# Earlier transposes of the normed block, and a one-slice cross sublayer in a new order

## The chip, the cores and the metric

One Trainium2 chip, one of its cores. The metric is the device time of the whole program in microseconds (us); lower is better. The core's engines run side by side and synchronise by semaphores: TensorE (PE; its weight loads are listed as PEld), VectorE (DVE), ScalarE (ACT), GpSimd (POOL), and SyncE (SP), which issues the loads of the weights.

## What is computed

Fourteen sublayers over 256 tokens of width 1024, in float32. Each ends with a residual and a layer norm over the whole row:

```
for layer in 0, 1:                      # first block, sublayers 0 to 5
    x = LN(a*x + mixer(x))              # "even" (mLSTM and a neighbourhood attention), then "odd" (differential)
    x = LN(a*x + cross(x, mem))         # 4 heads of 256: softmax(q k^T / 16) v, then @ wo  (1024 x 1024)
    x = LN(a*x + (silu(x@wg) * (x@wu)) @ wd)       # hidden width 2816
for layer in 0, 1:                      # second block, sublayers 6 to 13
    x = LN(a*x + 0.5 * swiglu(x))
    x = LN(a*x + merge(x))              # three gated branches
    x = LN(a*x + cross(x, mem_2))       # 4 heads of 128: wq 1024 x 512, wkv 1024 x 1024, wo 512 x 1024
    x = LN(a*x + 0.5 * swiglu(x))
```

The order is even, cross, ffn, odd, cross, ffn | ffn, merge, cross, ffn, ffn, merge, cross, ffn. All projections keep float32 accuracy: each operand is split into a high part (fp32r) and a low remainder, and a product is three matmuls (high x low, low x high, high x high).

## The kernel before

**Tiles of weights.** A weight tile is 128 x 2048 elements (1 MB; a few are smaller). SyncE loads it to one of three raw buffers, in one fixed order, and waits with a load until the tile three places before it is split. ScalarE makes the high part (wh, L1069) and VectorE the low part (wl, L1510) of each, in the same order. Most tiles go through a ring of three places (wh, wl); a place is rewritten once the tile three before in the ring is used. Beside the ring there are slots in memory that is otherwise free at a time: front, side (in oh, ol), back (in hh, hl), mem and note (em and en). They hold the opening tiles of the next sublayer. ScalarE and VectorE split ahead of need: `get(name)` on either splits every tile up to the one two ring places (`look=PARTS - 1`) behind the newest that was in the ring, or in use, when TensorE's program wrote the result `name`, and then waits for the result. Slot tiles between them in the order are split on the way.

**The end of a sublayer** (`out_proj`). The output is y = (activations) @ W, in two halves of 512 columns, and k runs over 128 rows of W; a step is a tile of four k. The last three steps (in the one-slice cross two steps, which are all) are held: the products of the first block of 128 tokens for all held tiles come first, then those of the second block. So the first block's residual and norm, on VectorE, run beside the second block's products. Then the normed block is transposed on TensorE (`x_to_T`, eight transposes of 128 x 128 for a block, in two halves of four) and split to xh (ScalarE, L1099) and xl (VectorE, L1543).

**The opening of a sublayer** (`enter`), where it isn't a cross sublayer: products of the first block with two or three opening tiles, then of the second block. Nine openings: after the two cross sublayers of the first block (two slices of wo, c = 2), after the two of the second block (one slice, c = 1) and after five ffn. Ffn and merge have three opening tiles, odd has two. Since every opening tile is taken with the first block's parts first, `await_parts` stands ahead of both blocks.

**Cross sublayers.** The memory is transposed and its keys and values are projected at the end of the sublayer before (`cross_kv`). In the one-slice form (sublayers 8 and 12) there are one tile of each half of the queries, two of the keys, two of the values (k 0 to 3 and 4 to 7), two of wo. `cross` then projects the first queries, computes scores of unit 0, projects the second queries, and runs four units (heads) through a pipeline: scores, negated maximum on VectorE (L1651), exponentials on ScalarE (L1144), division on VectorE (L1661), transposes of the probabilities, values, parts oh and ol.

VectorE's residual of the first block begins with `o = get(name, ...)` with a look of two ring tiles, and its second half with a split of all opening tiles:

```
if half and j + 1 in entry_last:
    split_to(entry_last[j + 1])
o = get(name, 0 if t and (half or by_block) and not cross_after(j) else PARTS - 1)
```

Of the kernel before, what the change touches and what calls it, by code (L numbers as in the profile page):

```python
# [9 lines left out]
ALU = mybir.AluOpType  # L10
# [3 lines left out]
P = 128  # L14
D = 1024
KC = D // P
# [4 lines left out]
FFN = 2816  # L21
HC = FFN // P
PAIRS = (HC - 4) // 2
ALPHA = 4.0 ** 0.25
EPS = 1e-5
NEG = -1e30
# [57 lines left out]
def program(nc, ctx, A, out, LAST=14):  # L84
# [160 lines left out]
    weight_tiles = []  # L245
    ring = []
    free_after = {}
    entry_last = {}
    where = {}
    uses = [0] * 8  # L250
    given = [0] * 8
# [85 lines left out]
    def _(pe):  # L337
# [134 lines left out]
        def y_products(j, t, half, k0, kc, sh, sl, tile, ks=None):  # L472
            h, l = tile
            name = ("y", j, t, half)
            o = ps[where[name][0]]
            for k in ks or range(k0, min(k0 + 4, kc)):
                tok = slice(t * P, t * P + P)
                three(o[:, :], sh[:, k, tok], sl[:, k, tok], h[:, k - k0, :], l[:, k - k0, :], k == 0, k == kc - 1,
                      name if k == kc - 1 else None)
# [7 lines left out]
        def out_proj(j, W, kc, sh, sl, need=None, steps=None):  # L487


            if steps is None:  # L490
                steps = [(half, k0) for half in range(2) for k0 in range(0, kc, 4)]
            held = 0 if cross_after(j) else min(PARTS, len(steps))
            enters = j + 1 < LAST and not cross_after(j)
            early, late = entry_slots(j) if enters else ([], [])
            tiles = []
            for half, k0 in steps[:len(steps) - held]:
                if need:
                    need(min(k0 + 4, kc))
                y_step(j, W, half, k0, kc, sh, sl)
                if (half, k0) in ((0, 4), (0, 12)) and enters:  # L500
                    tiles.append(order_entry(j + 1, len(tiles), early.pop(0)))
                if half == 0 and k0 + 4 >= kc and cross_after(j):
                    mem_start[j + 1] = len(halves)
                    mem_to_T(j + 1)
            if enters and kc == HC:
                free_after["back"] = len(ring) - 1
                if early:
                    tiles.append(order_entry(j + 1, len(tiles), early.pop(0)))
            held_tiles = []
            for half, k0 in steps[len(steps) - held:]:  # L510
                if need:
                    need(min(k0 + 4, kc))
                held_tiles.append(y_tile(j, W, half, k0, kc))
                while early or late and (half, k0) == steps[-1]:
                    tiles.append(order_entry(j + 1, len(tiles), (early or late).pop(0)))
                if (half, k0) == steps[-1]:
                    if enters:
                        entry_last[j + 1] = tiles[-1]
                y_products(j, 0, half, k0, kc, sh, sl, held_tiles[-1])
            for i, (half, k0) in enumerate(steps[len(steps) - held:]):  # L520
                ks = list(range(k0, min(k0 + 4, kc)))
                if i == held - 1 and enters:
                    y_products(j, 1, half, k0, kc, sh, sl, held_tiles[i], ks[:-1])
                    x_to_T(j + 1, [0])
                    ks = ks[-1:]
                y_products(j, 1, half, k0, kc, sh, sl, held_tiles[i], ks)
                owed[0] += 1
            if cross_after(j):
                cross_kv(j + 1)
            elif enters:  # L530
                enter(j + 1, tiles)
# [74 lines left out]
        def cross_kv(j):  # L606
# [2 lines left out]
            await_parts()  # L609
            for n in range(2 * c):  # L610
                proj_T(("xk", j, n), [wkv[:, n * S:n * S + S]], KC, mh, ml)
            for half in range(c):
                for k0 in (0, 4):
                    if k0 and half == c - 1:
# [2 lines left out]
                           "acc" if half == c - 1 else "work")  # L617
            for slot in ("mem", "note"):
                free_after[slot] = len(ring)

        def transposed_probs(u, src):
            pe.wait_ge(sig("prob_ready"), unit[0] + u + 1)
# [7 lines left out]
        def cross(j):  # L630
            _, blk, layer, _ = SUB[j]
            _, wq, _, wo, c = cross_of(blk, layer)
            await_parts()
            for n in range(c):
                proj_T(("xq", j, n), [wq[:, n * S:n * S + S]], KC, xh, xl)
# [419 lines left out]
    def _(act):  # L1055
# [60 lines left out]
        def norm(j):  # L1116
            for t in range(TB):
                ahead(("y", j, 1 if cross_after(j) else t, 1), PARTS - 1 if t == 0 or cross_after(j) else 0)
                if j + 1 in entry_last:
# [34 lines left out]
        def softmax(n_units, biased, after, beside=None):  # L1154
# [21 lines left out]
                    after(t - 3)  # L1176
            unit[0] += n_units

        def cross(j):
            c = cross_of(SUB[j][1], 0)[4]  # L1180
            base = unit[0]

            def query(n):
                name = ("xq", j, n)
# [309 lines left out]
    def _(dve):  # L1494
# [76 lines left out]
        def out_proj(j):  # L1571

            _, _, c = norm_of(j)

            def residual(t, half):
                f = slice(half * 512, half * 512 + 512)
                name = ("y", j, t, half)
                if half and j + 1 in entry_last:
                    split_to(entry_last[j + 1])
# [38 lines left out]
            if cross_after(j):  # L1618
                c = cross_of(SUB[j + 1][1], 0)[4]
                for half in range(c):  # L1620
                    if half == c - 1:
                        x_to_T(j + 1)
                    for t in range(TB):
                        name = ("xv", j + 1, t, half)
                        o = get(name)
# [28 lines left out]
        def normalise(g, biased):  # L1654
# [3 lines left out]
            else:  # L1658
# [2 lines left out]
            dve.tensor_tensor(two(prob[:, g % 2, :]), two(prob[:, g % 2, :]), along(rden[:, g % 2, 0:2], S),  # L1661
                              ALU.mult).then_inc(sig("prob_ready"), 1)

        def cross(j):
            c = cross_of(SUB[j][1], 0)[4]
            base = unit[0]

            def after(u):
                name = ("O", base + u)
# [674 lines left out]
```

## Time and profile before

| | |
|---|---|
| three runs | 2366.25, 2378.0, 2381.45 us |
| median | 2378.0 us |
| profiled execution: its time | 2377.74 us |
| profiled execution: span of its instructions | 2375.9 us |
| mean granted clock of TensorE | 0.987 |
| TensorE busy | 2267.1 us (95%) |
| VectorE busy | 1457.9 us (61%) |
| ScalarE busy | 1053.9 us (44%) |
| DMA | 411.68 MB, mean 173 GB/s |

The span is from the first to the last instruction. TensorE's busy time overlaps in itself: a matmul is listed from its start to its modelled end, while the next starts before that. A granted clock of 1.00 is 2.4 GHz, 0.50 is 1.2 GHz.

### The profile page before, as it was taken

Reading aid. Unit: us, or ns where it says so; the run is one execution under the profiler, and the core shown is the slowest. Engines: PE = TensorE matmul, PEld = TensorE weight load, DVE = VectorE, ACT = ScalarE, POOL = GpSimd, SP = SyncE. Lnnn points to the kernel's source line nnn. Section 1 sums busy time; section 2 is a strip of 40 time slices with the busy share of each in tenths; the row PEclk is TensorE's granted clock in tenths of the full one; section 3 lists DMA queues with packets and bytes.
Section 4 is the critical chain, followed back from the end, with each engine's and each line's share of the span. In section 5 each row is a group of like instructions: output and inputs, shape, how many; then the busy total and the mean of one; then the engine's idle time right before and its main releaser. Section 6 shows DMA issues by size and latency. Waiting matters only on the chain. (4 is left out here: it accounts for less than half of the span.)

```text
span 2375.9 us, 38020 instructions
## 1 busy us (share of the span) xinstructions
PE 2267.1 (95%) x15963; PEld 2079.4 (88%) x15963; DVE 1457.9 (61%) x1708; ACT 1053.9 (44%) x1237; POOL 113.1 (5%) x179
## 2 busy tenths in 40 slices
PE   8979999998999999999999998999999999998998
PEld 8858899877888998997998987997997898986996
DVE  6676555568756555555764676555555765676454
ACT  4534444445453443443455444443443455444442
POOL 2130000000000000000011000000000002000000
PEclk9999999999999999999999999999999999999999
DMA  8545556643445665555642663565566553564553
GB/s 251 167 119 197 172 160 196 225 138 107 173 147 178 195 222 161 185 200 168 199 145 83 206 213 125 178 203 187 178 195 209 169 161 100 171 233 137 178 187 115
DMA packets 337753, 411.68 MB, mean 173 GB/s; under 512 B 11244, under 2 KB 269480, under 8 KB 337456
## 3 DMA queue, kind: packets, MB, share of 16 engines
q1 hardware_dynamic: 328480, 377.18, 49.1%
q0 software_dynamic: 9104, 32.06, 4.4%
q8 instruction: 128, 2.10, 0.4%
q14 instruction: 41, 0.34, 0.0%
HBM read 406.31 MB, written 5.00 MB: 173 GB/s over the span
## 5 line engine op out<-in xcount | busy, mean ns | idle before, releaser
L1510 DVE TENSOR_TENSOR wl<-raw,wh 128x2048 fp32r<-128x2048 f32 (+2 forms) x351 | 764.7, 2184 | 521.6 <-ACT wh L1069 423.2
L342 PE MATMUL bank<-xl,wh 128*128 128x256 f32 x3136 | 878.8, 280 | 4.8 <-issue 3.5
L342 PE MATMUL bank<-xh,wl 128*128 128x256 f32 x3136 | 872.6, 278 | 0.0
L342 PE MATMUL bank<-xh,wh 128*128 128x256 f32 x3136 | 872.5, 278 | 0.0
L1069 ACT ACTIVATE wh<-raw 128x2048 fp32r<-128x2048 f32 (+2 forms) x351 | 637.3, 1821 | 332.3 <-PE bank L342 295.8
L342 PEld LDWEIGHTS bank<-xl,wh 128*128 128x128 f32 x3136 | 592.1, 189 | 13.6 <-issue 12.5
L342 PEld LDWEIGHTS bank<-xh,wl 128*128 128x128 f32 x3136 | 593.6, 189 | 0.6 <-issue 0.2
L342 PEld LDWEIGHTS bank<-xh,wh 128*128 128x128 f32 x3136 | 590.8, 188 | 0.0
L342 PE MATMUL bank<-wl,hh 128*128 128x512 f32 x528 | 206.2, 390 | 4.6 <-DVE wl L1510 4.6
L342 PE MATMUL bank<-wh,hh 128*128 128x512 f32 x528 | 205.5, 389 | 0.0
L342 PE MATMUL bank<-wh,hl 128*128 128x512 f32 x528 | 205.5, 389 | 0.0
L342 PEld LDWEIGHTS bank<-wl,hh 128*128 128x128 f32 x528 | 99.1, 188 | 26.4 <-issue 6.2
L342 PEld LDWEIGHTS bank<-wh,hh 128*128 128x128 f32 x528 | 99.1, 188 | 20.5
L342 PEld LDWEIGHTS bank<-wh,hl 128*128 128x128 f32 x528 | 99.1, 188 | 20.0
L1215 ACT ACTIVATE gate_s<-bank 128x512 f32<-128x512 f32 x54 | 32.3, 598 | 184.4 <-PE bank L342 184.4
L342 PE MATMUL bank<-wl,oh 128*128 128x512 f32 x224 | 91.3, 407 | 11.1 <-ACT oh L1099 10.2
L342 PE MATMUL bank<-wh,oh 128*128 128x512 f32 x224 | 89.3, 399 | 0.0
L342 PE MATMUL bank<-wh,ol 128*128 128x512 f32 x224 | 89.1, 398 | 0.0
L1099 ACT ACTIVATE xh<-bank 128x512 fp32r<-128x512 f32 x56 | 30.4, 598 | 112.6 <-PE bank L342 112.6
L1543 DVE TENSOR_TENSOR xl<-bank,xh 128x512 fp32r<-128x512 f32 x56 | 36.1, 686 | 66.9 <-ACT xh L1099 66.9
L2166 POOL DMA_DIRECT2D gb<-in_ln_g x14 | 7.6, 539 | 1376.0 <-DVE x L1614 1376.0
L342 PEld LDWEIGHTS bank<-wl,oh 128*128 128x128 f32 x224 | 43.4, 194 | 22.1 <-ACT oh L1099 11.9
(362 smaller groups left out, 3149.3 us busy)
## 6 DMA issues: line engine op xcount, KB each, us to landing
raw<-in_ffn_w_in SPq DMA_DIRECT2D x80, 1024.0 KB, 5.2
raw<-in_w_mix_in SPq DMA_DIRECT2D x56, 1024.0 KB, 5.4
raw<-in_ffn_w_gu SPq DMA_DIRECT2D x40, 1024.0 KB, 5.2
raw<-in_ffn_w_out SPq DMA_DIRECT2D x40, 1024.0 KB, 5.0
raw<-in_ffn_w_down SPq DMA_DIRECT2D x20, 1024.0 KB, 5.0
raw<-in_mem_wkv SPq DMA_DIRECT2D x16, 1024.0 KB, 6.3
raw<-in_even_w_in SPq DMA_DIRECT2D x14, 1024.0 KB, 7.2
raw<-in_odd_w_in SPq DMA_DIRECT2D x12, 1024.0 KB, 5.3
```

The costliest lines, as they stand in the source:

```text
L342: ins = pe.transpose(o, a, b) if transpose else pe.matmul(o, a, b, start=start, stop=stop)
L1069: act.activation(part_of(t, 0), raw_tile(t), ACT.Copy).then_inc(sig("w_high"), 1)
L1099: act.activation(dst, src, ACT.Copy).then_inc(sig("part_high"), 1)
L1215: free(("gate", j, q), act.activation(gate_s[:, q % 2, :], o[:, :], ACT.Silu))
L1510: dve.tensor_tensor(part_of(t, 1), raw_tile(t), part_of(t, 0).bitcast(F32), ALU.subtract)\
L1543: ins = dve.tensor_tensor(dst, src, hi.bitcast(F32), ALU.subtract)
L2166: pool.dma_start(gb[:, i, :], v.partition_broadcast(P)).then_inc(sig("gains_loaded"), 16)
```

## The change

`out_proj` on TensorE's side: the opening tiles are ordered elsewhere. After an ffn the back tile comes behind the second held tile (before: ahead of all held tiles). In a two-slice cross mem comes behind the first held tile and note behind the second (before: both behind the first). In a one-slice cross mem, note and front all come behind the second, last output tile (before: mem and note between the two). There the first held tile's products wait for their output parts k by k. The transposes of the first normed block come when three k of the second block's products are left (`BESIDE = 3`; before: one k).

`enter`: the transposes of the second block come ahead of the third opening tile of the first block (before: behind it). With two opening tiles nothing changes.

`cross_kv`, one slice: the transposes of x come behind both key tiles and ahead of the first value tile; the second value tile moves to the cross sublayer. `single_cross`: both query tiles, four scores one after the other, the second value tile, transposes of all four units, then all four outputs. Probabilities use prob and logit, transposed ones probT and bm, so that each unit has a buffer. ScalarE begins with a small exponential. ScalarE splits the mem tile between the transposed probabilities and the outputs; VectorE splits mem and note behind the outputs.

```
@@ out_proj on TensorE
             if enters and kc == HC:
                 free_after["back"] = len(ring) - 1
-                if early:
-                    tiles.append(order_entry(j + 1, len(tiles), early.pop(0)))
             held_tiles = []
-            for half, k0 in steps[len(steps) - held:]:
-                if need:
+            for i, (half, k0) in enumerate(steps[len(steps) - held:]):
+                gradual = need and kc == 4 and len(held_tiles) == 0
+                if need and not gradual:
                     need(min(k0 + 4, kc))
                 held_tiles.append(y_tile(j, W, half, k0, kc))
-                while early or late and (half, k0) == steps[-1]:
-                    tiles.append(order_entry(j + 1, len(tiles), (early or late).pop(0)))
-                if (half, k0) == steps[-1]:
+                if i + 1 == held:
+                    for slot in early + late:
+                        tiles.append(order_entry(j + 1, len(tiles), slot))
                     if enters:
-                        entry_last[j + 1] = tiles[-1]
-                y_products(j, 0, half, k0, kc, sh, sl, held_tiles[-1])
+                        entry_tiles[j + 1] = tiles
+                elif early and (i or kc != HC) and kc != 4:
+                    tiles.append(order_entry(j + 1, len(tiles), early.pop(0)))
+                y_products(j, 0, half, k0, kc, sh, sl, held_tiles[-1], need=need if gradual else None)
+            todo = sum(min(k0 + 4, kc) - k0 for _, k0 in steps[len(steps) - held:])
             for i, (half, k0) in enumerate(steps[len(steps) - held:]):
-                ks = list(range(k0, min(k0 + 4, kc)))
-                if i == held - 1 and enters:
-                    y_products(j, 1, half, k0, kc, sh, sl, held_tiles[i], ks[:-1])
-                    x_to_T(j + 1, [0])
-                    ks = ks[-1:]
-                y_products(j, 1, half, k0, kc, sh, sl, held_tiles[i], ks)
+                for k in range(k0, min(k0 + 4, kc)):
+                    if todo == BESIDE and enters:
+                        x_to_T(j + 1, [0])
+                    y_products(j, 1, half, k0, kc, sh, sl, held_tiles[i], [k])
+                    todo -= 1
                 owed[0] += 1
@@ enter
-                if t == 1:
-                    x_to_T(i, [1])
                 await_parts()
                 for m, n in enumerate(tiles):
...
+                    if t == 0 and m == 2:
+                        x_to_T(i, [1])
...
+                if t == 0 and len(tiles) == 2:
+                    x_to_T(i, [1])
@@ cross_kv
+            if c == 1:
+                x_to_T(j)
+                proj_N([("xv", j, t, 0) for t in range(TB)], wkv, 512, 512, KC, mh, ml, [0], "acc")
+                return
@@ TensorE
+        def single_cross(j):
...
+            await_parts()
+            for n in range(2):
+                proj_T(("xq", j, n), [wq[:, n * S:n * S + S]], KC, xh, xl)
+            await_read(("xk", j, 0), ("xk", j, 1))
+            base = len(halves)
+            for u in range(4):
+                await_read(("xq", j, u // 2))
+                o = take(("S", unit[0] + u))
+                for tb in range(TB):
+                    mm(o[:, tb * S:tb * S + S], xq[:, u, tb * P:tb * P + P], xk[:, u, :], True, True,
+                       ("S", unit[0] + u) if tb == 1 else None)
+            proj_N([("xv", j, t, 0) for t in range(TB)], wkv, 512, 512, KC, mh, ml, [4], "acc")
+            for slot in ("mem", "note"):
+                free_after[slot] = len(ring)
+            for u in range(4):
+                transposed_probs(u, lambda tb, kb: (prob, logit)[u // 2][:, u % 2, tb * S + kb * P:tb * S + kb * P + P])
+            await_read(("xv", j, 0, 0), ("xv", j, 1, 0))
+            for u in range(4):
+                await_read(("T", unit[0] + u))
+                o = take(("O", unit[0] + u), "acc")
+                for kb in range(TB):
+                    mm(o[:, 0:S], xv[:, kb, u * P:u * P + P], (probT, bm)[u // 2][:, u % 2, kb * S:kb * S + S],
+                       kb == 0, kb == 1, ("O", unit[0] + u) if kb == 1 else None)
+                parts(("O", unit[0] + u))
+            unit[0] += 4
+            out_proj(j, wo, 4, oh, ol, need=lambda k: await_parts(base + k))
@@ ScalarE
+        def single_cross(j):
+            act.activation(psum_e[:, 0, 3:4], mv[:, 0, 2:3], ACT.Exp, scale=0.0)
...
+            split_to(entry_tiles[j + 1][0])
...
@@ VectorE
+        def single_cross(j):
...
+            neg_max(unit[0], False)
+            for u in range(1, 4):
+                neg_max(unit[0] + u, False)
+                normalise_unit(u - 1)
+            normalise_unit(3)
+            for t in range(TB):
+                name = ("xv", j, t, 0)
+                o = get(name)
+                free(name, dve.tensor_copy(xv[:, t, 0:512], o[:, :]))
...
+            split_to(entry_tiles[j + 1][1])
@@ out_proj on VectorE, residual
-                if half and j + 1 in entry_last:
-                    split_to(entry_last[j + 1])
+                if half and j + 1 in entry_tiles:
+                    split_to(entry_tiles[j + 1][1 if single and t == 0 else -1])
```

## Rows read from the trace of the kernel before

**Rows 1.** The page: granted clock of TensorE in 40 slices, tenths
```profile
PEclk9999999999999999999999999999999999999999
```

**Rows 2.** Waits of TensorE: us in total, times, longest us
```profile
PE bank L342 <- ACT xh L1099: 25.3, 19, 1.7
...
PE bank L342 <- DVE wl L1510: 5.1, 6, 1.5
```

**Rows 3.** Groups of TensorE by form: count | busy, mean ns | idle before
```profile
L342 PE MATMUL bank<-front_l,xh 128*128 128x256 f32 x96 | 27.2, 283 | 5.4 <-ACT xh L1099 5.4
...
L342 PE MATMUL bank<-em_l,xh 128*128 128x256 f32 x64 | 19.3, 302 | 10.4 <-ACT xh L1099 10.4
...
L342 PE MATMUL bank<-front_l,xh 128*128 128x512 f32 x24 | 9.9, 412 | 8.0 <-ACT xh L1099 8.0
```

**Rows 4.** Time line of TensorE, opening of sublayer 6: start, us, [idle before]
```profile
919.77 1.03 PE L342 MATMUL bank<-ident,x 128*128 128x128 f32 x8
920.56 0.48 PE L342 MATMUL bank<-wl,hh 128*128 128x512 f32 x1
...
922.49 0.35 PE L342 MATMUL bank<-front_l,xh 128*128 128x256 f32 x1 [0.99 <-ACT xh L1099]
...
931.05 1.03 PE L342 MATMUL bank<-ident,x 128*128 128x128 f32 x8
933.77 0.36 PE L342 MATMUL bank<-front_l,xh 128*128 128x256 f32 x1 [1.69 <-ACT xh L1099]
```

**Rows 5.** Time line of VectorE, the same opening
```profile
913.84 0.69 DVE L1581 SCALAR_TENSOR_TENSOR z<-x,bank 128x512 f32<-128x512 f32 x1 [3.22 <-PE bank L342]
...
918.03 0.75 DVE L1614 SCALAR_TENSOR_TENSOR x<-z,mv,gb 128x512 f32<-128x512 f32 x1
921.10 1.29 DVE L1543 TENSOR_TENSOR xl<-bank,xh 128x512 fp32r<-128x512 f32 x2 [2.32 <-ACT xh L1099]
```

**Rows 6.** Time line of VectorE and of TensorE, held tiles of sublayer 5
```profile
902.11 2.29 DVE L1510 TENSOR_TENSOR hl<-raw,hh 128x2048 fp32r<-128x2048 f32 x1 [6.20 <-ACT hh L1069]
...
906.75 0.47 PE L342 MATMUL bank<-wl,hh 128*128 128x512 f32 x1 [1.53 <-DVE wl L1510]
```

**Rows 7.** Waits of TensorE, 1400 to 1460 us, sublayer 8
```profile
PE bank L342 <- DVE prob L1661: 5.0, 2, 4.2
PE bank L342 <- ACT xq L1186: 3.2, 2, 2.3
PE bank L342 <- ACT oh L1099: 1.0, 1, 1.0
```

**Rows 8.** Time line of TensorE: first output product, first opening product of sublayer 9
```profile
1445.51 0.47 PE L342 MATMUL bank<-wl,oh 128*128 128x512 f32 x1 [1.05 <-ACT oh L1099]
...
1459.81 0.35 PE L342 MATMUL bank<-em_l,xh 128*128 128x256 f32 x1 [0.84 <-ACT xh L1099]
```

**Rows 9.** Time line of VectorE, end of sublayer 8
```profile
1444.98 0.42 DVE L1543 TENSOR_TENSOR ol<-bank,oh 128x256 fp32r<-128x256 f32 x1 [0.53 <-ACT oh L1099]
...
1448.98 2.28 DVE L1510 TENSOR_TENSOR wl<-raw,wh 128x2048 fp32r<-128x2048 f32 x1
1451.18 0.68 DVE L1581 SCALAR_TENSOR_TENSOR z<-x,bank 128x512 f32<-128x512 f32 x1
...
1456.81 0.75 DVE L1614 SCALAR_TENSOR_TENSOR x<-z,mv,gb 128x512 f32<-128x512 f32 x1
```

**Rows 10.** Windows: us, TensorE busy, granted clock, DMA share, GB/s
```profile
1433.00:1439.00 6.00, 3.34 (x10) 0.50 1.10 342
1440.00:1445.00 5.00, 3.72 (x20) 1.00 0.01 2
1460.00:1463.40 3.40, 3.40 (x18) 0.51 0.00 0
```

**Rows 11.** Issues of loads, whole span and 906 to 911 us: median to landing
```profile
raw<-in_ffn_w_in SPq DMA_DIRECT2D x80, 1024.0 KB, 5.2
...
raw<-in_ffn_w_in SPq DMA_DIRECT2D x3, 1024.0 KB, 7.6
```

More of the change, by code:

```diff
@@ L23 @@
 PAIRS = (HC - 4) // 2
+BESIDE = 3
 ALPHA = 4.0 ** 0.25
@@ L247, in program @@
     free_after = {}
-    entry_last = {}
+    entry_tiles = {}
     where = {}
@@ L470, in y_tile, with y_products @@
             return weights([W[k0 * P:min(k0 + 4, kc) * P, half * 512:half * 512 + 512]], min(4, kc - k0))
-        def y_products(j, t, half, k0, kc, sh, sl, tile, ks=None):
+        def y_products(j, t, half, k0, kc, sh, sl, tile, ks=None, need=None):
             h, l = tile
@@ L476, in y_products @@
             for k in ks or range(k0, min(k0 + 4, kc)):
+                if need:
+                    need(k + 1)
                 tok = slice(t * P, t * P + P)
@@ L619, in cross_kv @@
                 free_after[slot] = len(ring)
+        def single_cross(j):
+            _, blk, layer, _ = SUB[j]
+            _, wq, wkv, wo, _ = cross_of(blk, layer)
+            await_parts()
[24 more added lines that the diff above has]
+            out_proj(j, wo, 4, oh, ol, need=lambda k: await_parts(base + k))
         def transposed_probs(u, src):
@@ L632, in cross @@
             _, wq, _, wo, c = cross_of(blk, layer)
+            if c == 1:
+                single_cross(j)
+                return
             await_parts()
@@ L1118, in norm @@
                 ahead(("y", j, 1 if cross_after(j) else t, 1), PARTS - 1 if t == 0 or cross_after(j) else 0)
-                if j + 1 in entry_last:
-                    split_to(entry_last[j + 1])
+                if j + 1 in entry_tiles:
+                    split_to(entry_tiles[j + 1][-1])
                 wait("var_ready", 2 * j + t + 1)
@@ L1177, in softmax @@
             unit[0] += n_units
+        def single_cross(j):
+            act.activation(psum_e[:, 0, 3:4], mv[:, 0, 2:3], ACT.Exp, scale=0.0)
+            for n in range(2):
+                name = ("xq", j, n)
+                o = get(name)
+                free(name, act.activation(xq[:, 2 * n:2 * n + 2, :], two(o[:, :]), ACT.Copy, scale=float(P ** -0.5)))
+            for u in range(4):
+                g = unit[0] + u
+                src = get(("S", g))
+                wait("neg_max", g + 1)
+                free(("S", g), exps(g, src, (prob, logit)[u // 2][:, u % 2, :]))
+            for u in range(4):
+                name = ("T", unit[0] + u)
+                o = get(name)
+                free(name, act.activation((probT, bm)[u // 2][:, u % 2, :], o[:, :], ACT.Copy))
+            split_to(entry_tiles[j + 1][0])
+            for u in range(4):
+                name = ("O", unit[0] + u)
+                o = get(name)
+                high(name, oh[:, u, :], o[:, 0:S])
+            unit[0] += 4
+            out_proj(j)
         def cross(j):
@@ L1181, in cross @@
             base = unit[0]
+            if c == 1:
+                single_cross(j)
+                return
             def query(n):
@@ L1573, in out_proj @@
             _, _, c = norm_of(j)
+            single = SUB[j][:2] == ("cross", 2)
             def residual(t, half):
@@ L1577, in residual @@
                 name = ("y", j, t, half)
-                if half and j + 1 in entry_last:
-                    split_to(entry_last[j + 1])
+                if half and j + 1 in entry_tiles:
+                    split_to(entry_tiles[j + 1][1 if single and t == 0 else -1])
                 o = get(name, 0 if t and (half or by_block) and not cross_after(j) else PARTS - 1)
@@ L1622, in out_proj @@
                         x_to_T(j + 1)
+                    if c == 1:
+                        return
                     for t in range(TB):
@@ L1662, in normalise, with normalise_unit @@
                               ALU.mult).then_inc(sig("prob_ready"), 1)
+        def single_cross(j):
+            def normalise_unit(u):
+                g = unit[0] + u
+                p = (prob, logit)[u // 2][:, u % 2, :]
+                await_read(("S", g))
+                link(dve.reciprocal(rden[:, g % 2, 0:2], psum_e[:, g % 2, 0:2]))
+                dve.tensor_tensor(two(p), two(p), along(rden[:, g % 2, 0:2], S), ALU.mult)\
+                   .then_inc(sig("prob_ready"), 1)
+            neg_max(unit[0], False)
[5 more added lines that the diff above has]
+                name = ("xv", j, t, 0)
+                o = get(name)
+                free(name, dve.tensor_copy(xv[:, t, 0:512], o[:, :]))
+            for u in range(4):
+                name = ("O", unit[0] + u)
+                o = get(name)
+                low(name, ol[:, u, :], o[:, 0:S], oh[:, u, :])
+            split_to(entry_tiles[j + 1][1])
+            unit[0] += 4
+            out_proj(j)
         def cross(j):
@@ L1666, in cross @@
             base = unit[0]
+            if c == 1:
+                single_cross(j)
+                return
             def after(u):
```

## Prediction

> **What bounds the kernel now.** I read the page first, then the waits of TensorE, its groups, and last the time line of the three kinds of place that the diff touches. TensorE's granted clock is near full in all forty slices [rows 1], and the page has TensorE busy for 95% of the span (the table above): what can be won is the time in which it stands still or runs at its lower clock. The list of its waits [rows 2] gives the size: 25.3 us in 19 waits for high halves of transposed activations (xh), and 5.1 for low halves of weights. The groups [rows 3] tell where the first lie: 10.4 us before tiles of the mem slot (four cross sublayers that open an ffn), 5.4 before 256 columns of the front slot (two ffn that open an ffn), 8.0 before 512 columns of it (three openings of a mixer): 23.8 us at nine openings. No large wait names a DMA, so the weight stream isn't the bound.
>
> **One opening, looked at closely** [rows 4]. Eight transposes start at 919.77 and take 0.79 us to issue (until 920.56); one k, three products of 0.23, follows; the opening tile could start at 921.25 and starts at 922.49. The view says 0.99, since it counts from the last product's modelled end; in issue time the wait costs **1.24**. The second block's transposes start at 931.05, have issued by 931.84, and the next tile starts at 933.77: **1.93** (listed 1.69). VectorE's rows [rows 5] give the two spans of the step: from the residual's start (913.84) to the second half of x (918.03 + 0.75 = 918.78) 4.94 us, and from the transposes' start to the last low half (921.10 + 1.29 = 922.39) 2.62.
>
> **Transposes three k ahead of the end.** Behind them now lie nine products, 9 x 0.23 = 2.07, with the 0.79 of issue 2.86 us, over the 2.62 needed: the wait goes entirely, if x is there at the earlier place. After an ffn the held tiles hold 10 k, so the second block has run 7 k x 0.69 = 4.8 us when the transposes come; x needs 4.94, which leaves 0.1 to wait. In the two-slice cross 9 k lie ahead, 6.2 us, and only the front tile's split (2.3) comes between the residuals; nothing to wait. Seven openings (five after ffn, two after the two-slice cross) x 1.24 = 8.7, less 5 x 0.1: **8.2 us**. The other two are below.
>
> **Second block's transposes ahead of the third opening tile.** Two tiles of 2.85 us (three fill the 8.56 from 922.49 to 931.05 [rows 4]) lie ahead: 5.7 us after the products end, against 4.94 for x. After a cross both residuals of the block come then, 1.45 more, from the last low half on, which is about where the queue arrives. The third tile hides the 2.62. Eight openings have a third tile, 8 x 1.93 = **15.4 us**. The odd mixer has two and keeps its wait.
>
> **The back tile two places later.** Four ffn open with three tiles. TensorE waits there for the low half of the first held tile [rows 6]: VectorE stood 6.20 us before the back slot's low half, with the held tile queued behind it. The list's 5.1 us in 6 waits [rows 2] is this four times (1.53 in the row, and smaller) and two specks; in issue time 0.16 more each, so **5.2 us**. With back behind the second held tile, the first needs only a slot freed two tiles earlier, and back is split beside its products. The last held tile, half as large, queues behind back but is due two tiles of 2.8 us later. If back's load were late, the residual behind it would be too (rival E).
>
> In the two-slice cross the note tile moves behind one held tile: the same splits within the same stretch, nothing. Together **28.8 us**; I take 28.5.
>
> **The one-slice cross (sublayers 8 and 12): what goes.** Ahead of the output products (1445.51 [rows 8]) TensorE waits 5.0 us for probabilities, 3.2 for queries and 1.0 for output parts [rows 7]: 9.2 in five waits, 1.2 more in issue time. From 1433 to 1439 the granted clock is 0.50, that is 1.2 GHz, over 3.34 us busy [rows 10], worth 1.7. The cause is in the order: mem, note and the second output tile are split in one run, and ScalarE's query copy and VectorE's maximum queue behind them. In the new order the four scores follow both queries, and the value slice of 5.6 us (24 x 0.23) covers the softmax. **What comes:** ScalarE splits the second output tile only on asking for the first transposed probabilities (1.9), VectorE then its low half (2.3), and only then copies the two value blocks (2 x 0.7): 5.6 us from the last exponential. VectorE's four maxima and four divisions of some 0.7 each and the exponentials between them end about 1.7 before the slice does, and sixteen transposes take another 1.6 (0.79 for eight [rows 4]). A new wait of about 2.2, from 0 up to the whole 5.6. Net 9.2 + 1.2 + 1.7 - 2.2: the output products start about 10 us sooner, and the last low half is ready at 1436.1 instead of 1445.40 [rows 9].
>
> **Where that goes.** The first block's residual looks two ring tiles ahead. When it is recorded the first output tile is the newest, so two ahead is the next section's first gate tile, which stands behind mem, note and front in the order of splitting. The kernel before shows this wait: the gate tile's low half starts at 1448.98 and the residual only at its end, 1451.18, 5.8 us after the last low half (1444.98 + 0.42 = 1445.40) [rows 9]. Now mem and note stand there too, and worse, the gate tile's load may start only when mem, three tiles before it, is split. From the last low half: mem 2.3; a load, 5.2 alone and 7.6 where three overlap [rows 11], 6.4 with one behind it; ScalarE 1.9, VectorE 2.3 [rows 9], steps between 0.2: 13.1 us, 7.3 more than before. So x comes 9.3 - 7.3 = 2.0 sooner, not 10. TensorE does its five k and then stands about **9 us** at the transposes. Behind their second half come nine products, 2.5 us with the issue, where the row shows 2.25 (1457.56 to 1459.81 [rows 8, 9]): the opening tile starts **1.7 sooner**. The trace has no stand of 9 us; the nearest is 4.2 [rows 7], after which 1.2 GHz lasted some 3.9 us of work, worth 2.1 with what is beside it [rows 10]. I charge 2.1 here and 1.0 for the outputs behind the 2.2 us wait (bounds 0 and 3.3, their whole length). Against it goes the lower clock from 1460 to 1463.4 [rows 10], 1.6 in one of the two, 0.8 each. Each such cross: -1.7 + 2.1 + 1.0 - 0.8 = **0.6 slower**, between -8 (nothing of the chain bites) and +8 (7.6 for the load, 1.2 GHz for 10 us); its 1.93 for the second block is in the 15.4 already.
>
> The Trainium skill, "TensorE: Matmul & The Clock Gate", Part 4: PE-mode transpose, says that transposes don't count as busy for the clock gate as other matmuls do. Against this change it would mean that sixteen transposes in a row and the wait behind them look like one idle stretch, and that the outputs always run at the lower level. The row is less plain: from 1440 to 1445, with two sets of such transposes, the granted clock is 1.00 [rows 10]. By the rule the two sublayers would cost 2 x 2.3 more, and the sum be 2355.
>
> **Sum.** The profiled execution took 2377.7 for a span of 2375.9, 0.3 below the median of the three runs (2378.0). 2377.7 - 28.5 + 2 x 0.6 = 2350.4; I give **2350**.
>
> **Rivals.** (B) The one-slice cross keeps its gain: the gate tile's load is early, or the residual doesn't look so far. For it: TensorE's waits there are real. Against it: the order of splits in [rows 9]. 2377.7 - 28.5 - 2 x 8 = 2333. (C) The openings give half back: x isn't there at the earlier place, or the next gate tiles aren't split when TensorE arrives 4 us sooner. For it: 0.1 us of margin at five places. Against it: no wait stands there now, and the splits move along. 28.5 becomes 14: 2364. (D) The cross is dear, 8 us each by its upper bound: 2365. (E) Slower, by the back tile. It and the last held tile are now split just ahead of the first block's second residual. As I place them both are done by 907.6 on the scale of [rows 6], and the residual starts at 913.84 less 1.7: 4.5 us of room. A load later than that would be paid in full at four exits, first in x, then at the transposes. It decides the sign from 4.5 + 28 / 4 = 11.5 us late; at 13 the kernel takes 2383. The slowest loads in view take 7.6 [rows 11], 2.4 over the usual.
>
> **Chances.** Forecast 0.50 (its own range 2344 to 2357), B 0.15, C 0.16, D 0.15, E 0.04. From B to D, leaving out the outer part of each: **2336 to 2365**. A measurement of this kernel tells from no change about 1%, 24 us, so faster means under 2354. Of the forecast 0.85 lies below it, all of B, little of C and D: 0.58 faster, 0.38 same, 0.04 slower.
>
> **What the profile after would show.** The waits for xh fall from 25.3 us to 2 to 4 (the start and the odd mixer); those for wl go. In sublayers 8 and 12 stand one wait of about 2 us for the copied values before the outputs, then one of some 9 for x before its transposes, with mem, note, front and a gate tile split ahead of the first residual, and a lower clock behind it. The prediction is wrong if waits of over 0.5 for x stand at the ffn exits (C), or no long wait in the one-slice cross (B).

## The result, and the profile after

| | before | after |
|---|---|---|
| median of four runs | 2372.12 us | 2344.16 us |
| lowest to highest | 2363.32 to 2381.45 us | 2339.09 to 2349.29 us |
| profiled execution: time, span | 2377.74, 2375.9 us | 2343.55, 2341.8 us |
| TensorE's mean granted clock | 0.987 | 0.987 |

After over before: **0.9895**, 95% interval 0.987 to 0.9921, so 19 to 31 us gained. The prediction was 2350 within 2336 to 2365. It was made from three runs of the kernel before with a median of 2378.0; the fourth, 2363.32, brought that to 2372.12. As a gain, it said 27.6 us, and 28.0 was measured.

The page's row of the granted clock is the same as in [rows 1]: all forty slices at nine tenths or more.

The waits of TensorE in the changed kernel, us in total, times, longest (beside [rows 2]):

```profile
PE bank L343 <- DVE x L1684: 18.1, 4, 8.7
...
PE bank L343 <- DVE wl L1579: 3.4, 2, 1.7
PE bank L343 <- ACT xh L1142: 3.2, 2, 1.7
PE bank L343 <- DVE xv L1754: 3.1, 2, 1.5
```

The wait for high halves fell from 25.3 us in 19 to 3.2 in 2, the start and the odd mixer. A wait for x takes its place with 18.1 us, two of them of 8.7; in the kernel before it was 2.0 in all, 0.8 at most. And there is still a wait for low halves of weights, though no longer at the back tiles.

**An opening without a stand.** The time line of TensorE at the opening of sublayer 6, in the changed kernel (beside [rows 4]): start, us.

```profile
909.01 1.09 PE L343 MATMUL bank<-ident,x 128*128 128x128 f32 x8
...
912.01 0.28 PE L343 MATMUL bank<-front_l,xh 128*128 128x256 f32 x1
...
917.67 1.04 PE L343 MATMUL bank<-ident,x 128*128 128x128 f32 x8
...
921.37 0.28 PE L343 MATMUL bank<-front_l,xh 128*128 128x256 f32 x1
```

No row has an [idle]. From the first opening product to the second block's first one it takes 9.36 us, where [rows 4] have 11.28. VectorE shows how narrow the first step is: its second half of x starts at 908.63 and takes 0.75, while the transposes have started at 909.01 on the first half. With five k instead of three this would not do (below).

**The one-slice cross.** TensorE in sublayer 8 of the changed kernel (beside [rows 8]):

```profile
1413.71 1.97 PE L343 MATMUL bank<-probT,xv 128*128 128x256 f32 x8 [1.53 <-DVE xv L1754]
...
1417.05 0.58 PE L343 MATMUL bank<-wl,oh 128*128 128x512 f32 x1
...
1435.02 1.12 PE L343 MATMUL bank<-ident,x 128*128 128x128 f32 x4 [8.75 <-DVE x L1684]
1436.47 1.11 PE L343 MATMUL bank<-ident,x 128*128 128x128 f32 x4 [0.33 <-DVE x L1684]
...
1440.37 0.28 PE L343 MATMUL bank<-em_l,xh 128*128 128x256 f32 x1
```

VectorE in the same stretch (beside [rows 9]):

```profile
1417.92 0.42 DVE L1612 TENSOR_TENSOR ol<-bank,oh 128x256 fp32r<-128x256 f32 x1 [0.44 <-ACT oh L1142]
1418.27 2.28 DVE L1579 TENSOR_TENSOR em_l<-raw,em_h 128x2048 fp32r<-128x2048 f32 x1
1420.47 2.29 DVE L1579 TENSOR_TENSOR en_l<-raw,en_h 128x2048 fp32r<-128x2048 f32 x1
1422.67 2.28 DVE L1579 TENSOR_TENSOR front_l<-raw,front_h 128x2048 fp32r<-128x2048 f32 x1
1427.82 2.29 DVE L1579 TENSOR_TENSOR wl<-raw,wh 128x2048 fp32r<-128x2048 f32 x1 [2.87 <-issue]
1430.03 0.68 DVE L1651 SCALAR_TENSOR_TENSOR z<-x,bank 128x512 f32<-128x512 f32 x1
```

and ScalarE's row for the gate tile (wh) between them:

```profile
1425.82 1.91 ACT L1112 ACTIVATE wh<-raw 128x2048 fp32r<-128x2048 f32 x1 [4.39 <-DMA raw<-in_ffn_w_in]
```

The four tiles mem, note, front and gate are all split ahead of the first residual, and ScalarE stands 4.39 us for the gate tile's load. That load was issued at 1420.64, just behind mem's low half (1420.55). The whole chain, last low half (1418.34) to residual (1430.03), is 11.7 us.

Windows of the changed kernel: us, busy time of TensorE, PEld, VectorE, ScalarE and GpSimd, granted clock, DMA share, GB/s (beside [rows 10]):

```profile
1413.70:1417.00 3.30, 3.29 (x15) 2.94 (x16) 0.85 (x2) 2.22 (x4) 0.00 (x0) 1.00 1.05 286
1429.10:1439.30 10.20, 3.94 (x13) 3.16 (x14) 8.71 (x15) 1.40 (x3) 0.00 (x0) 0.50 0.53 171
```

The outputs run at the full 2.4 GHz after sixteen transposes and a wait of 1.53 us; the lower clock stands behind the wait of 8.75 us, over the first 4.3 us of work.

**Where 34.1 us of span went.** Stages are measured between two fixed points of TensorE's time line (first product with the memory, called the keys; first opening product; for the end of an opening, the first product with the last opening tile for the second block after a cross, and with the first one after an ffn), in the profiled run of either kernel:

| stages | before | after | change |
|---|---|---|---|
| openings of four ffn after a cross, each | 17.1 (18.6 in sublayer 9) | 15.1 | -9.6 in all |
| block 0 to block 1, four openings of three tiles after an ffn, each | 11.28, 11.07, 11.28, 10.96 | 9.36, 9.04, 9.36, 9.04 | -7.8 |
| odd mixer's | 8.39 | 8.22 | -0.2 |
| five ffn, from their opening to the next | 868.86 | 857.45 | -11.4 |
| one-slice cross, keys to opening | 70.73, 70.75 | 68.51, 68.46 | -4.5 |
| two-slice cross, keys to opening | 110.43, 109.83 | 111.24, 111.33 | **+2.3** |
| even mixer and the start | 188.05 | 183.49 | -4.6 |
| rest | | | +1.6 |

The line of the even mixer isn't the change's: this stage took 182.2 to 191.9 us over the twelve profiled executions of the study. In the line of the ffn, two of the five took another pace after than before (last section), one some 3.7 us shorter for it and one as much longer. Since such spreads move a single span by several us, the experiments with one run are read by the stages that their edit touches, not by their span. An ffn at like pace repeats to 0.02 us (167.68 to 167.70 in the kernels that leave it alone). The stages from keys to opening don't repeat so well. The two-slice one took 110.5 to 111.4 us in the twelve places of six kernels whose code is the same there (the changed one and five experiments), mean 110.9; the one-slice one took 68.3 to 69.4 in eight places of four, mean 68.9. So what a single run says of a cross is good to half a microsecond or so, and of the kernel before there is only one trace.

### The profile page after: what moved, and what is told of

Same layout as the page of the kernel before. It is cut to its first block and busy times, and to the rows that moved or that the text cites. A ratio compares the mean times of both kernels' runs of the same rounds, so it can differ in the third digit from the quotient of the medians.

```text
span 2341.8 us, 38028 instructions
## 1 busy us (share of the span) xinstructions
PE 2258.9 (96%) x15963; PEld 2080.4 (89%) x15963; DVE 1453.7 (62%) x1708; ACT 1055.1 (45%) x1239; POOL 116.0 (5%) x179
## 5 line engine op out<-in xcount | busy, mean ns | idle before, releaser
L343 PE MATMUL bank<-wl,oh 128*128 128x512 f32 x224 | 92.3, 412 | 11.7 <-issue 4.4
L1165 ACT ACTIVATE mv<-mv 128x1 f32<-128x1 f32 x28 | 5.7, 203 | 126.5 <-DVE mv L1673 126.5
```

Source lines behind the costliest of these rows:

```text
L343: ins = pe.transpose(o, a, b) if transpose else pe.matmul(o, a, b, start=start, stop=stop)
```

## The experiments

Ten kernels, all edits of the changed kernel. "Before" was run beside each on the same chip.

**The position of the transposes.** The first edit puts them back to one k before the end:

```diff
-BESIDE = 3
+BESIDE = 1
```

> The first block's transposes stand one k before the end again; the rest as changed. Theory: at seven openings the wait for xh of 0.99 us comes back, 1.24 each in issue time, 8.7 us; in the two one-slice crosses the opening tile starts 1.3 sooner, since the transposes are the late step there and only one k follows them: together some 6 us above 2344. Rival (the gain at the openings is all of the second block's transposes): the time line to the opening tiles doesn't change.

One run: 2351.45 us. The waits of TensorE, in the kernel with BESIDE = 1:

```profile
PE bank L343 <- ACT xh L1142: 10.1, 9, 1.7
```

Two of the nine are the old two, so seven openings wait 1.0 each, as in [rows 4]. The ffn's exit stage is 168.78 us instead of 167.70: +1.08. The one-slice cross takes 68.69 and 67.39 us, next to 68.51 and 68.46: there the stand for x is ahead of the transposes. The 1.3 us that had been expected show in one of the two at most, and both openings behind them are longer (15.65 and 16.09 us against 15.1), so nothing is gained. The two-slice cross takes 111.7 and 111.9, 0.8 over its mean of 110.9.

The second goes the other way, to five k:

```diff
-BESIDE = 3
+BESIDE = 5
```

> The first block's transposes stand five k before the end instead of three. Theory (x is ready 4.9 us after the residual begins, and three k is just at that edge after an ffn): at five ffn exits TensorE waits for x for about 1.5 us more before the transposes, in the two-slice cross less than 1, in the one-slice cross 1.4 more; nothing is won behind them, since nine products covered the way already: 10 to 13 us above 2344. Rival (there is slack at three k): under 4 us.

One run: 2355.91 us. TensorE at an ffn's exit, in the kernel with BESIDE = 5:

```profile
478.93 0.66 PE L343 MATMUL bank<-ident,x 128*128 128x128 f32 x4 [0.18 <-DVE x L1684]
480.38 0.66 PE L343 MATMUL bank<-ident,x 128*128 128x128 f32 x4 [0.79 <-DVE x L1684]
```

Now x is late. All waits for x are 26.4 us in 16, against 18.1 in 4. Where pace and clock were alike the exits took 1.1 to 1.4 us more (169.06 against 167.70; 178.53 against 177.19). The transposes can't be earlier than the norm: of the three places that were tried, three k is the one where both waits are nil.

**The second block's transposes**, back behind the third tile:

```diff
@@ enter
-                    if t == 0 and m == 2:
-                        x_to_T(i, [1])
...
-                if t == 0 and len(tiles) == 2:
+                if t == 0:
                     x_to_T(i, [1])
```

> The second block's transposes stand behind all opening tiles of the first block again; the rest as changed. Theory: eight waits for xh of 1.69 us come back, 1.93 each in issue time, 15.4 us above 2344. Rival (what is waited for is VectorE's norm, not the way through the transposes): waits of another length, and less than 8 us.

One run: 2355.61 us; the waits, and one of the places, in that kernel:

```profile
PE bank L343 <- ACT xh L1140: 16.7, 10, 1.7
```
```profile
931.00 0.36 PE L343 MATMUL bank<-front_l,xh 128*128 128x256 f32 x1 [1.69 <-ACT xh L1140]
```

Eight waits of 1.69 are back. Block 0 to block 1 takes 11.21 us instead of 9.36: 1.85 x 8 = 14.8.

**The back tile**, ahead of the held tiles again:

```diff
@@ out_proj
                 free_after["back"] = len(ring) - 1
+                if early:
+                    tiles.append(order_entry(j + 1, len(tiles), early.pop(0)))
```

> The back tile stands ahead of all held tiles after an ffn again; the rest as changed. Theory (the waits for wl at four ffn exits come from back's place alone): waits of 1.53 us twice and 0.76 twice come back, 5.2 us in issue time. Rival (they went since TensorE's other waits moved it against the splits): they don't come back, or at other sizes.

One run: 2351.91 us. Waits, and the first held tile of sublayer 5, in that kernel:

```profile
PE bank L343 <- DVE wl L1581: 8.0, 6, 1.7
```
```profile
906.25 0.47 PE L343 MATMUL bank<-wl,hh 128*128 128x512 f32 x1 [1.53 <-DVE wl L1581]
```

The wait of [rows 6] is back, and four exits are longer, by 1.78 (169.48 against 167.70) twice and by 0.84 (174.39 against the 173.55 of other kernels with the same code there, at the same pace) twice: 5.2 us.

**The note tile of the two-slice cross.** The changed kernel's time line has a wait of 1.69 at 282.84, in sublayer 1, the first cross sublayer (and one of 1.70 in sublayer 4), which the kernel before hasn't. VectorE there, in the changed kernel:

```profile
278.20 2.29 DVE L1579 TENSOR_TENSOR en_l<-raw,en_h 128x2048 fp32r<-128x2048 f32 x1 [1.10 <-ACT en_h L1112]
280.41 2.28 DVE L1579 TENSOR_TENSOR wl<-raw,wh 128x2048 fp32r<-128x2048 f32 x1
```

and in the kernel before:

```profile
272.96 2.29 DVE L1510 TENSOR_TENSOR em_l<-raw,em_h 128x2048 fp32r<-128x2048 f32 x1 [1.96 <-ACT em_h L1069]
275.17 2.28 DVE L1510 TENSOR_TENSOR en_l<-raw,en_h 128x2048 fp32r<-128x2048 f32 x1
277.37 2.28 DVE L1510 TENSOR_TENSOR wl<-raw,wh 128x2048 fp32r<-128x2048 f32 x1
```

Before, mem, note and a held tile are split in one run while both engines have nothing else to do. With the note tile one place later the splitting engines reach it only after the next output parts, and the last held tile, which TensorE needs in the middle of the held products, queues behind it. The edit puts the note tile alone back, in the two-slice cross:

```diff
                 elif early and (i or kc != HC) and kc != 4:
                     tiles.append(order_entry(j + 1, len(tiles), early.pop(0)))
+                    while early and kc != HC:
+                        tiles.append(order_entry(j + 1, len(tiles), early.pop(0)))
```

> In the two-slice cross the note tile stands behind the first held tile again, as in the kernel before; everything else as changed. Theory (the two waits of 1.69 us for wl that the changed kernel has before its last held tile come from note standing just ahead of that tile in the order of splitting): both waits go, 1.94 each in issue time, 3.9 us less from the output products to the opening tile of sublayers 2 and 5. Rival (they come from the later load of the last held tile, or from the transposes' new place): they stay.

One run: 2332.68 us. The waits of TensorE from 255 to 300 us in it no longer name wl (0.7 for issue and 0.6 for probabilities are all). Keys to opening: 108.57 and 108.67 us, 2.7 less each than in the one trace of the changed kernel, below the kernel before (110.43, 109.83) too. Over all traces the difference is smaller: six places in the three kernels with this edit (this one and the last two below) have 108.6 to 109.4, mean 109.0, against 110.9 in the twelve without it. That is **2.0 less** each, where 1.94 was expected. So the tile's move had cost what the earlier transposes gained here, and more.

**The stand for x.** Three edits ask whether the chain through the gate tile's load makes it. The first lets the residuals of a one-slice cross look at no ring tile ahead, on both splitting engines:

```diff
@@ VectorE, residual
-                o = get(name, 0 if t and (half or by_block) and not cross_after(j) else PARTS - 1)
+                o = get(name, 0 if (t and (half or by_block) or single) and not cross_after(j) else PARTS - 1)
@@ ScalarE, norm
-                ahead(("y", j, 1 if cross_after(j) else t, 1), PARTS - 1 if t == 0 or cross_after(j) else 0)
+                single = SUB[j][:2] == ("cross", 2)
+                ahead(("y", j, 1 if cross_after(j) else t, 1),
+                      PARTS - 1 if t == 0 and not single or cross_after(j) else 0)
```

> In the one-slice cross the first block's residual and ScalarE's step before its root no longer split ahead to the next section's gate tile; mem and note are still split before the residual, front before the second block's. Theory (the 8.7 us before the transposes of x are the look-ahead chain mem, load of the gate tile 5.2, its two splits): from the last low half (1418.35) two splits of 2.3 end at 1422.8, so the residual starts 7.3 sooner, the wait falls to 1 to 2 us, and the 10 us at the granted clock 0.50 go or shrink. The opening tile starts 8 to 9 sooner in each of the two, less some 1.5 for front's low half now between the second block's residuals: 13 to 18 us below the changed kernel's 2344. Rival (what holds the norm is VectorE's own work behind the outputs, or the load of another tile): the wait stays over 5 us and the time within 5 us of 2344.

Four runs: 2320.89 us (2316.97 to 2326.6), **0.979** of the kernel before (0.977 to 0.9809). VectorE, in the kernel with no look ahead:

```profile
1416.36 2.28 DVE L1581 TENSOR_TENSOR em_l<-raw,em_h 128x2048 fp32r<-128x2048 f32 x1
...
1420.76 0.68 DVE L1653 SCALAR_TENSOR_TENSOR z<-x,bank 128x512 f32<-128x512 f32 x1
...
1430.64 2.29 DVE L1581 TENSOR_TENSOR front_l<-raw,front_h 128x2048 fp32r<-128x2048 f32 x1
1432.85 0.68 DVE L1653 SCALAR_TENSOR_TENSOR z<-x,bank 128x512 f32<-128x512 f32 x1
```

and TensorE:

```profile
1425.75 0.66 PE L343 MATMUL bank<-ident,x 128*128 128x128 f32 x4 [1.37 <-DVE x L1686]
...
1436.59 0.63 PE L343 MATMUL bank<-ident,x 128*128 128x128 f32 x4 [0.96 <-DVE x L1686]
```

The residual starts 4.3 us after the last low half (1416.44) instead of 11.7, the stand is 1.37 instead of 8.75, and the four transposes behind it take 0.66, not 1.12: after this stand the clock was still full. Keys to opening: 59.81 and 61.41 us, against 68.5. A part comes back: front is now split between the second block's residuals, so the second transposes wait (0.96), and the openings take 17.10 and 15.89 us instead of 15.1. By stages the two sublayers win 13 us, the low end of the 13 to 18 expected. The span is 17 shorter, and the slower pace of one ffn in the run of the changed kernel (last section) is the other 3.6. The median is 23 lower, more than expected; the 6 between span and median have no place.

The second edit leaves the look as it is and only puts mem's low half ahead of the outputs' low halves:

```diff
@@ VectorE, single_cross, behind the copies of the values
+            split_to(entry_tiles[j + 1][0])
```

> VectorE splits mem's low half ahead of the four low halves of the outputs instead of behind them; the look-ahead stays as changed. Theory A (the chain is mem split, then the load of the gate tile, then its two splits): the load starts 3 us sooner, the outputs' low halves up to 1.5 later and not on the chain, and the wait of 8.7 us before x's transposes falls by 2 to 3. Theory B (the sum of VectorE's splits behind the outputs is what counts, the load is hidden): the wait stays within 1 us, or grows by what the outputs are late.

One run: 2334.84 us. TensorE's wait for x, and ScalarE's for the gate tile's load, in that kernel:

```profile
PE bank L343 <- DVE x L1684: 9.9, 4, 4.7
```
```profile
1417.99 1.92 ACT L1112 ACTIVATE wh<-raw 128x2048 fp32r<-128x2048 f32 x1 [0.96 <-DMA raw<-in_ffn_w_in]
```

Mem's raw buffer is free earlier, so the load starts earlier: ScalarE stands 0.96 for it instead of 4.39, and TensorE 4.56 instead of 8.75. All tiles are still split ahead of the residual. Of the stand some 4 us, more than the 2 to 3 expected, were therefore the load, started only when mem was split, and the rest the splits. Keys to opening: 65.94 and 65.24, 2.6 and 3.2 less.

The third parts the two halves of the change to this sublayer: the old computation (scores, softmax, values unit by unit, both value tiles in `cross_kv`) with the new order of tiles.

```diff
@@ cross_kv on TensorE
-            if c == 1:
-                x_to_T(j)
-                proj_N([("xv", j, t, 0) for t in range(TB)], wkv, 512, 512, KC, mh, ml, [0], "acc")
-                return
...
@@ cross on TensorE; the same on ScalarE and VectorE
-            if c == 1:
-                single_cross(j)
-                return
...
```

> The one-slice cross computes in the order of the kernel before (scores between the queries, both value tiles ahead, units in a pipeline, transposes of x between the value tiles), while mem, note and front stay behind both output tiles and all else is as changed. Theory (the new order of computing takes some 10 us off the way to the outputs, and the look-ahead behind them takes most of it back): without it the outputs start some 4 to 5 us later than in the changed kernel, since here too no mem or note split stands in the softmax, and the opening tile as much later, 4 to 5 us in each of two sublayers, 8 to 10 in all. Rival (the place of the tiles is all that counts, the order of computing nothing): the same time from the keys to the opening tile as in the changed kernel, 68.5 us.

One run: 2355.62 us. Waits of TensorE in that kernel:

```profile
PE bank L343 <- DVE x L1674: 21.3, 4, 10.3
PE bank L343 <- DVE prob L1721: 14.6, 12, 2.4
```

Keys to opening: 75.35 and 75.73 us. The size was missed by 2 to 3 us. The new tile order (with the rest of the change to `out_proj`) costs 4.8 over the kernel before (70.7), and the new computation gives 6.6 to 7.0 back, by the mean of 68.9 or by the changed kernel's own 68.5. Together they are the 1.9 to 2.2 that were gained. The stand for x doesn't need the new computation, since it is there (10.3) with the old one too. The converse, the new computation with the old order of tiles, was not run.

**Together.** The two edits that won, on one kernel, five runs each from here on:

> The changed kernel with the look-ahead of the one-slice cross off (mem and note split before the residual, no gate tile) and note behind the first held tile in the two-slice cross. Theory: both gains add, 13 to 17 us and 4 to 5 us below 2344, 2324 or a little less, and a ratio to the kernel before of 0.976 to 0.980. Rival (one takes the place of the other, or the look-ahead's gain was that run's luck): a ratio over 0.982.

2320.77 us (2312.44 to 2323.08), 0.9782 (0.9757 to 0.9807). Against 0.979 without the note tile's edit this is no measured gain, though its stages show it: 109.27 and 108.70 us, where the kernel with the first edit alone had 111.24 and 110.67.

Last, the wait for the copied values: VectorE's look in front of them goes from two ring tiles to one, so that the second output tile is split behind the copies.

```diff
@@ VectorE, single_cross
-                o = get(name)
+                o = get(name, 1)
```

> As the kernel with both edits, and VectorE copies the value blocks before it splits the second output tile. Theory (TensorE's 1.5 us wait before the outputs is that split of 2.3 us ahead of the copies): the wait goes and the outputs start 1.5 to 1.8 us sooner in both one-slice crosses; the split then stands ahead of the outputs' low halves, so that the last of these is at most 1 us sooner: 0 to 3 us less in all. Rival (the wait is for the copies themselves): it stays, and the time too.

2313.11 us (2309.16 to 2317.23), **0.976** (0.9739 to 0.9781). Waits of TensorE in that kernel:

```profile
PE bank L343 <- DVE x L1688: 6.3, 8, 1.1
...
PE bank L343 <- DVE ol L1616: 3.3, 4, 1.5
```

The row for xv is gone. Keys to opening: 58.04 and 58.05 us (61.40 and 59.80 without), 1.2 of it given back in one opening. That is 3.9 us by stages, a little over the 0 to 3 expected; the medians differ by 7.7, but the two kernels' runs overlap. It has the lowest median of the study: 57 us below the kernel before, twice what the change brought.

## Why the prediction held, step by step

The likeliest case came. As a time, 2344 lies at the lower edge of its own range (2344 to 2357), because the median of the kernel before fell by 5.9 us with its fourth run; as a gain, 27.6 us were predicted and 28.0 measured. Neither sign of being wrong showed: no wait for x stands at an ffn exit (rival C), and the long wait in the one-slice cross is there (B).

- **Transposes three k ahead:** 8.2 us over seven openings predicted. The five ffn give 1.08 each, 5.4 (1.14 each predicted); the two-slice crosses 0.8 each by the kernel with BESIDE = 1, and 1.2 by the kernels with the note tile put back beside the kernel before. The margin of 0.1 us for x was real: at five k x is late.
- **Second block's transposes:** 15.4 predicted, 14.8 by the experiment.
- **Back tile:** 5.2 predicted, 5.2 measured. Rival E, its load late for the residual, did not come.
- **Note tile of the two-slice cross:** "the same splits within the same stretch, nothing". This failed. It costs 2.0 us in each, 3.9 in all. The count of splits is the same, but the two engines had free time before the move that they don't have after it, and what queues behind the moved tile, the last held tile, was not named.
- **One-slice cross:** 0.6 slower each predicted. Against the kernel before it is 2.2 to 2.3 faster up to its opening in the changed kernel's trace, 1.9 by the mean of eight, and 0.8 each for the lower clock behind it in one of the two, as charged. So 3.2 to 3.6 each were mis-sized. The mechanism was the predicted one: the output products 11.2 us sooner after the keys (45.19 against 56.43; about 10 predicted), a first wait, 1.53 for the copied values (2.2), then the stand, 8.75 (9), behind four splits and a load. What was off, all on one side: the outputs' clock (charged 1.0, the window of 1413.7 to 1417 shows 1.00, so nothing); the chain from the last low half, 11.7 instead of 13.1, because ScalarE could start on the gate tile 5.2 us after its load was issued and not 6.4; the last low half itself 0.5 sooner; the lower clock behind the stand, about 1.8 instead of 2.1 (transposes to opening 5.02 us without the wait between, against 3.22 in the kernel without look ahead). That makes 3.2.
- **The rule on transposes and the clock gate** (the Trainium skill, "TensorE: Matmul & The Clock Gate", Part 4: PE-mode transpose), by which transposes don't count as busy as other matmuls do, would have had the outputs at the lower level. The runs don't bear it out here: sixteen transposes in a row and 1.53 us of idle were followed by a granted clock of 1.00.

The two misses, 3.9 us too little charged for the note tile and 6.4 to 7.2 too much for the one-slice cross, partly cancel. That is luck: the sum was closer than its terms. Of the rivals, B (the cross keeps its gain) was wrong about this kernel, but is what it becomes with no look ahead: 59.8 to 61.4 us where the change has 68.5.

## What to carry to other kernels

When an order of splits or loads is changed, follow not only the moved tile but the one right behind it, and ask whether the engine was free at the old place: a move within the same stretch with the same count of operations still cost 2.0 us. When work is reordered to come sooner, look at what the next consumer waits for in program order: a look two tiles ahead in front of a residual turned 11 us of earlier outputs into an 8.75 us stand, and taking the look away gave 7 to 9 of them back, of which the opening behind it took 0.8 to 2.0 again. A transpose (or any step whose result needs a copy and a split) wants behind it just as much other work as its way takes, and ahead of it the time that its input takes; here two k too few cost 1.1 us at an ffn's exit, and two too many 1.1 to 1.4.

## What the runs showed of the hardware

**Two paces at one clock.** Products of 256 columns started 0.118 us apart at the opening of sublayer 6 of the changed kernel (24 from 912.01 to 914.84), and 0.113 apart before sublayer 8's scores (22 from 1398.82 to 1401.31), with no gap and a granted clock of 1.00 in both. Whole stages differ so. The same stage of two like ffn in one run of the kernel with both first edits, from the second block's first opening product to the next opening:

```profile
920.75:1097.93 177.18, 177.18 (x1264) 166.73 (x1263) 98.27 (x75) 76.09 (x64) 0.00 (x0) 1.00 0.61 196
1624.84:1798.39 173.55, 173.55 (x1265) 163.09 (x1263) 98.27 (x75) 76.22 (x64) 0.00 (x0) 1.00 0.63 201
```

TensorE is busy throughout both, with the same products, yet one takes 3.63 us longer. Which stage is slow changes from run to run (in the last kernel the order is the other way round: 173.55 in sublayer 6, 177.18 in sublayer 10), so it isn't the edit. What sets it stays open. For a reader of single runs it means that spans differ by several us for nothing. The length of an ffn stage can be read to 0.1 once its pace is known; the stages of the cross sublayers differ by 1 us between kernels with the same code there.

**The clock after a stand.** At the end of the one-slice cross 1.37 us of idle left the transposes behind it at 0.66 us for four, 4.56 us and 8.75 us of idle both made them 1.11 to 1.12.
